# A fused decoder layer with its start, sample attention, norms and closing products rearranged

## The reference, cut to what matters

```
h   = rmsnorm(x, norm1_g) * (1 + sc1) + sh1        # sh, sc, gt: six parts of silu(c) @ ada_w + ada_b
z   = h @ w_in                                     # recurrent branch, queries, three K/V sets, gates
o_c = attention over compressed K/V (+ T5 bias)    # gelu(chunks of 32 rows @ cmp_w1) @ cmp_w2
o_s = attention over selected blocks,  o_w = attention over a window of 512
o_att = g0 * o_c + g1 * o_s + g2 * o_w             # sample requests read paged caches of 1,024 rows
mixed = concat(rmsnorm(o_lru), rmsnorm(o_att)) @ w_out
x   = x + gt1 * mixed
h2  = rmsnorm(x, norm2_g) * (1 + sc2) + sh2
x   = x + gt2 * peer_ffn(h2)                       # keys pick 16 of 16,384 experts per head
y   = rmsnorm(x, final_g)
```

## Time and profile before

| | us |
|---|---|
| median of 3 runs (lowest, highest) | 1961.47 (1959.98, 1966.07) |
| the profiled execution, its time | 1964.24 |
| its span, first to last instruction | 1962.6 |
| TensorE busy | 1802.6 (92%) |
| VectorE busy | 1327.0 (68%) |
| ScalarE busy | 647.5 (33%) |
| GpSimd busy | 337.4 (17%) |

### The profile page before, as it was taken

The page is one execution under the profiler, slowest core; times in us unless marked ns, Lnnn a source line. Parts: engine busy times, 40 slices in busy tenths (PEclk is TensorE's granted clock), DMA queues, the critical chain, the costliest instruction groups (busy, mean ns, idle before and its releaser), DMA issues.

```text
span 1962.6 us, 30207 instructions
## 1 busy us (share of the span) xinstructions
PE 1802.6 (92%) x11322; PEld 1670.6 (85%) x11322; DVE 1327.0 (68%) x2967; ACT 647.5 (33%) x1012; POOL 337.4 (17%) x362
## 2 busy tenths in 40 slices
PE   3889998757797999899999999999999999999996
PEld 2667785634586999899999999999999999999995
DVE  0310343347427778999999999995777777777775
ACT  1111332137313222333434334333333333333331
POOL 0301000000000000111123333432222222222220
PEclk9689998659998999999999999999999999999998
DMA  6573665230005322687679999998999999999981
GB/s 229 159 276 100 208 219 168 117 142 1 1 26 190 102 86 75 234 266 245 224 234 352 358 355 346 341 340 325 398 393 334 335 342 340 339 339 338 332 277 44
DMA packets 177773, 467.60 MB, mean 238 GB/s; under 512 B 20601, under 2 KB 91641, under 8 KB 175988
## 3 DMA queue, kind: packets, MB, share of 16 engines
q1 hardware_dynamic: 132788, 291.91, 42.8%
q0 software_dynamic: 44864, 174.14, 24.8%
HBM read 408.65 MB, written 64.14 MB: 241 GB/s over the span
## 4 chain that ended last, share of the span: by engine, by line
PE 83%; DVE 9%; DMA 4%; issue 2%; ACT 2%; SPq 0%; DVEq 0%; ACTq 0%; POOLq 0%
PE ps L1027 28%; PE ps L924 24%; PE ps L540 7%; PE ps L911 5%; PE ps L1008 4%; PE ps L873 3%; DMA arena<-rrows 1%; PE ps L592 1%; ACT arena L1061 1%; PE ps L563 1%; PE ps L849 1%; PE ps L549 1%; DMA cst<-in_rel_bias 1%; PE ps L841 1%; PE ps L898 1%
## 5 line engine op out<-in xcount | busy, mean ns | idle before, releaser
L1643 DVE TENSOR_TENSOR ul<-raw,uh 128x1024 fp32r<-128x1024 f32 x256 | 313.6, 1230 | 135.7 <-ACT uh L1061 117.5
L924 PE MATMUL ps<-hh,uh 128*128 128x392 f32 x1024 | 358.8, 350 | 5.8 <-DVE ul L1643 5.8
L1027 PE MATMUL ps<-ah,uh 128*128 128x392 f32 x1024 | 348.8, 341 | 2.7 <-DVE al L1848 2.7
L1027 PE MATMUL ps<-ah,ul 128*128 128x392 f32 x1024 | 350.9, 343 | 0.0
L1027 PE MATMUL ps<-al,uh 128*128 128x392 f32 x1024 | 350.2, 342 | 0.0
L924 PE MATMUL ps<-hl,uh 128*128 128x392 f32 x1024 | 350.0, 342 | 0.0
L924 PE MATMUL ps<-hh,ul 128*128 128x392 f32 x1024 | 349.0, 341 | 0.0
L1061 ACT ACTIVATE uh<-raw 128x1024 fp32r<-128x1024 f32 x256 | 270.3, 1056 | 116.4 <-PE ps L1027 106.1
L502 POOL DMA_INDIRECT xT<-in_u,gidx x128 | 148.2, 1158 | 591.1 <-DVE zg L1686 365.6
L502 POOL DMA_INDIRECT xT<-in_v,gidx x128 | 132.9, 1039 | 419.0 <-DVE vacc L1838 386.0
L924 PEld LDWEIGHTS ps<-hh,uh 128*128 128x128 f32 x1024 | 193.5, 189 | 8.7 <-DVE ul L1643 7.1
(11 more groups left out here) (326 smaller groups left out, 2270.8 us busy)
## 6 DMA issues: line engine op xcount, KB each, us to landing
raw<-in_uT SPq DMA_DIRECT2D x128, 512.0 KB
raw<-in_v SPq DMA_DIRECT2D x128, 512.0 KB
zs<-zbuf SPq DMA_DIRECT2D x128, 196.0 KB
gw<-stage POOLq DMA_DIRECT2D x28, 896.0 KB
gr<-gw SPq DMA_DIRECT2D x32, 784.0 KB, 9.0
zin<-zs SPq DMA_DIRECT2D x128, 196.0 KB
arena<-in_ada_w SPq DMA_DIRECT2D x32, 512.0 KB, 4.6
arena<-in_w_in SPq DMA_DIRECT2D x18, 512.0 KB, 4.4
```

The costliest lines, as they stand in the source:

```text
L924: last = mm(ps[:, bank, 0:DN], w[x][:, k * P:(k + 1) * P], m[:, k, G0:TOK], start=(k == 0 and x == 0 and m is hh), stop=(k == KD - 1 and x ...
L1027: last = mm(ps[:, dc, 0:DN], w[:, q, cols], m[:, q, :], start=(first and w is uh and m is ah), stop=(final and w is ul))
L1643: tt(ul[:, i % 4, :], raw[:, i % 4, :], uh[:, i % 4, :].bitcast(F32), SUB).then_inc(S["lo_done"], 1)
```

## The change

In the start, GpSimd's and SP's queues and TensorE's order are rearranged. The 55 bias products become eight, of which copies go out to memory (`obias`) and come back in shifted rows as `pbias`. SP loads 20 pages, GpSimd 44, the latter only after `ada_step(3)`. The replicated bias table `rbx` is made by a copy instead of a load. The eight products with `wgate` stand behind block 0 and use four column groups. Block 0 takes `h` chunk by chunk. `ohw`, the bias of the window, is loaded at block 5 instead of after block 17. `hidden_prompt(0)` stands behind `hidden_prompt(1)`. SP waits for `biasT` before it loads `wout`. Four norms (all but that of the recurrent branch) sum squares into four strips of 32 partitions, each for 128 prompt columns and 8 more (`SW` = 136), take inverse and root of 136 columns instead of 520, and spread the roots over all partitions by five products. The second norm goes chunk by chunk. The last three `down` steps are taken output by output, with the transposes in their middle.

```diff
+            load_head(1, 1)
...
-            load_head(1, 1)
...
-            load(rbx[0:32].rearrange("p (b h) -> p b h", h=NH),
-                 io["rel_bias"].rearrange("a (o h) -> a o h", o=1).to_broadcast([32, P // NH, NH]), S["tables_loaded"])
...
+            sp.wait_ge(S["ada_ready"], 3)
+            for n in range(2):
+                load(win_w[:, n * KD:(n + 1) * KD, :], io["w_in"][n], w_l[n])
...
-            sp.wait_ge(S["ada_ready"], 3)
-            for n in range(2):
-                load(win_w[:, n * KD:(n + 1) * KD, :], io["w_in"][n], w_l[n])
-            load(w1p, io["w1p"], S["w1k_loaded"])
-            load(posp, io["posp"], S["pos_loaded"])
...
-            load_pages(0, 16)
+            load_pages(0, 12)
+            load(w1p, io["w1p"], S["w1k_loaded"])
+            load(posp, io["posp"], S["pos_loaded"])
...
-                    load_pages(16, 32)
+                    load_pages(12, 16)
+                if n == 3:
+                    load_pages(16, 20)
+                if n == 5:
+                    load(ohw[0:33], io["ohw"], S["ohw_loaded"])
...
-            load(ohw[0:33], io["ohw"], S["ohw_loaded"])
...
             sp.wait_ge(S["sel_free"], 1)
+            sp.wait_ge(S["bias_loaded"], 16)
             load(wout, io["w_out"], S["wout_loaded"])
             load(xT[:, :, :], io["xT"], S["x_loaded"])
...
+            pool.wait_ge(S["act_init"], 3)
+            pool.dma_start(rscratch, rsb[0:NH]).then_inc(S["scratch_stored"], 16)
             pool.wait_ge(S["page_loaded"], 16)
-            pool.wait_ge(S["ada_ready"], 3)
-            for n in range(32, 64):
+            pool.wait_ge(S["ada_ready"], ADA_HEAD)
+            for n in range(20, 64):
...
+            ob = io["obias"]
+            for a in range(8):
+                pool.dma_start(bass.AP(ob.tensor, a * NH, [[64 * NH, 16], [8 * NH, 8], [1, NH]]),
+                               tofs[16 * a:16 * a + 16].rearrange("p (w h) -> p w h", h=NH)).then_inc(S["scratch_stored"], 16)
             rows = io["rrows"]
             pool.dma_start(rows.rearrange("p h c -> p (h c)"),
                            rscratch.rearrange("h (o c) -> o (h c)", o=1).to_broadcast([P, NH * 640])
                            ).then_inc(S["rows_stored"], 16)
+            pool.wait_ge(S["scratch_stored"], 16 * 9)
+            for a in range(8):
+                pool.dma_start(pbias[16 * a:16 * a + 16], bass.AP(ob.tensor, (7 - a) * NH, [[64 * NH, 16], [NH, QM], [1, NH]])
+                               ).then_inc(S["rows_stored"], 16)
...
+            def strip_sums(b, x, k, n):
+                for j in range(4):
+                    last = mm(ps[32 * j:32 * j + 32, b, 0:SW], ones[:, 0:32], x[:, k, j * P:j * P + SW],
+                              start=(k == 0), stop=(k == n - 1))
+                return last
+            def spread_roots(b, bs):
+                for j in range(4):
+                    mm(ps[:, b, j * P:(j + 1) * P], ident[:, 32 * j:32 * j + 1].to_broadcast([P, P]), roots[:, 0:P], start=True, stop=True)
+                mm(ps[:, bs, 256:256 + NB], ident[:, 96:97].to_broadcast([P, P]), roots[:, P:SW],
+                   start=True, stop=True).then_inc(S["roots_ready"], 1)
...
+                    pe.wait_ge(S["gather_k"], 16 * 20)
+                    pe.wait_ge(S["pages_k"], 16 * 44)
...
             for g in range(ADA_HEAD):
+                if g >= 1:
+                    turn_m9(g - 1)
+                if g == 2:
+                    pe.wait_ge(S["act_init"], 2)
+                    for k in range(KD):
+                        last = strip_sums(0, hT, k, KD)
+                    last.then_inc(S["sum_ready"], 1)
+                    pe.wait_ge(S["tables_loaded"], 80)
+                    mm(ps[0:NH, 2, 0:512], rb[0:33], ohd[0:33, 513:1025], start=True, stop=True)
+                    mm(ps[0:NH, 3, 0:128], rb[0:33], ohd[0:33, 1025:1153], start=True, stop=True)
+                    for w in range(KD):
+                        last = mm(ps[:, 3, P + w * NH:P + (w + 1) * NH], oha[0:33, w * P:(w + 1) * P], rb[0:33], start=True, stop=True)
+                    last.then_inc(S["pe_init"], 1)
+                if g == 3:
+                    pe.wait_ge(S["rstd_ready"], 1)
+                    spread_roots(1, 0)
                 pe.wait_ge(head_l[g % 3], 16 * (g // 3 + 1))
                 aw = ada_head[g % 3].rearrange("p (c k) i -> p c k i", k=KD)
                 ada_step(g, lambda k: aw[:, :, k, :], 512)
-                if g == 0:
-                    pe.wait_ge(S["tables_loaded"], 96)
-                    offset_bias(0)
-                    pe.wait_ge(S["act_init"], 2)
-                    two(0, lambda k: ones[:, :], lambda k: hT[:, k, :], range(KD)).then_inc(S["sum_ready"], 1)
-                    continue
-                turn_m9(g - 1)
-                if g == 3:
-                    pe.wait_ge(S["root_in"], 1)
-                    mm(ps[0:NH, 0, 0:512], rb[0:33], ohd[0:33, 513:1025], start=True, stop=True)
-                    mm(ps[0:NH, 1, 0:128], rb[0:33], ohd[0:33, 1025:1153], start=True, stop=True).then_inc(S["pe_init"], 1)
-                offset_bias(g)
...
+            def gate_strips():
+                pe.wait_ge(S["wgate_loaded"], 16)
+                pe.wait_ge(S["mt_done"], ADA_HEAD)
+                for kk in range(2):
+                    for h in range(2):
+                        for j in range(4):
+                            last = mm(ps[32 * j:32 * j + 32, 6 + h, 0:HALF], wgate[:, 2 * j + kk, :],
+                                      hT[:, 2 * j + kk, h * HALF:(h + 1) * HALF], start=(kk == 0), stop=(kk == 1))
+                last.then_inc(S["zg_ready"], 1)
...
+                for k in range(KD):
+                    if n == 0:
+                        pe.wait_ge(S["h_ready"], k + 1)
+                    for h in range(2):
+                        last = mm(ps[:, 2 * (n % 2) + h, 0:HALF], win_w[:, (n % 2) * KD + k, :],
+                                  hT[:, k, h * HALF:(h + 1) * HALF], start=(k == 0), stop=(k == KD - 1))
...
-                    last.then_inc(S["zg_ready"], 1)
+                    gate_strips()
+                if n == 1:
+                    gate_sums()
...
+            hidden_prompt(1, 7, 128)
+            pe.wait_ge(S["w1k_loaded"], 48)
+            hidden_prompt(0, 1, 160)
...
+            pe.wait_ge(S["gelu_ready"], 4)
             pe.wait_ge(S["att_dve"], 3)
...
-            hidden_prompt(0, 160)
...
-            for c in range(2):
-                project(c, range(4))
+            project(0, range(4))
             pe.wait_ge(S["mix_sq"], 1)
-            two(0, lambda k: ones[:, :], lambda k: hT[:, k, :], range(4)).then_inc(S["mix_sum"], 1)
+            for k in range(4):
+                last = strip_sums(0, hT, k, 4)
+            last.then_inc(S["mix_sum"], 1)
+            project(1, range(3))
+            pe.wait_ge(S["rstd_ready"], 3)
+            spread_roots(1, 0)
+            project(1, range(3, 4))
             project(2, range(4))
             pe.wait_ge(S["mix_ready"], 1)
...
+                if c >= 2:
+                    chunk_sums(x1sq, c - 2, 0, 0)
+            for k in range(KD - 2, KD):
+                chunk_sums(x1sq, k, 0, 0)
+            pe.wait_ge(S["rstd_ready"], 4)
+            spread_roots(2, 3)
...
+                    if ready is not None and k % 2 == 0:
+                        pe.wait_ge(ready, k // 2 + 1)
...
+            down(P - 4, 0)
+            for dc in range(KD):
+                cols = slice(dc * P, (dc + 1) * P)
+                for q in range(1, 4):
+                    if dc == 0:
+                        pe.wait_ge(S["lo_done"], 2 * P - 3 + q)
+                        pe.wait_ge(S["a_ready"], P - 3 + q)
+                    for w, m in ((uh, ah), (uh, al), (ul, ah)):
+                        last = mm(ps[:, dc, 0:DN], w[:, q, cols], m[:, q, :], start=False, stop=(q == 3 and w is ul))
+                last.then_inc(S["ff_ready"], 1)
+                if dc == 3:
+                    pe.wait_ge(S["acc_step"], P)
+                    pe.wait_ge(S["bank_free"], 2)
+                    for c in range(KD):
+                        last = pe.transpose(ps[:, c // 4, (c % 4) * P:(c % 4 + 1) * P], vacc[:, c * P:(c + 1) * P], ident[:, :])
+                    last.then_inc(S["pe_turned"], 1)
+            for k in range(KD):
+                chunk_sums(sq, k, KD, 2)
+            pe.wait_ge(S["rstd_ready"], 5)
+            spread_roots(3, 2)
...
-            act.wait_ge(S["h_ready"], 2 * KD)
-            fn(hh[:, :, :], h2T, ACT.Copy).then_inc(S["rounded"], 1)
...
+            for k in range(KD):
+                act.wait_ge(S["h_ready"], KD + k + 1)
+                fn(hh[:, k, :], h2T[:, k, :], ACT.Copy).then_inc(S["hh_ready"], 1)
...
+            link(cp(rbx[0:33].rearrange("p (b h) -> p b h", h=NH),
+                    rb[0:33].rearrange("p (o h) -> p o h", o=1).to_broadcast([33, P // NH, NH])))
...
+            shift_m(1)
+            dve.wait_ge(S["sum_ready"], 1)
```

(44 more changed lines are left out.)

195 lines of the change are left out of this document (86 added, 109 removed).

## The result

The changed kernel takes 1863.74 us (median of four runs, 1859.92 to 1866.52) against 1960.72 (1958.52 to 1966.07) in the same series: a ratio of 0.950, 95% interval 0.9472 to 0.9528, 97 us less. Forecast were 1862, range 1844 to 1884.

A forecast was written before the change was run, and what follows sets the result against it. TensorE, 83% of the chain, was taken as the bound, with gains only in the first 620 and last 30 us. Gains 40 + 35 + 7 + 5 + 13 = 100 gave 1862 us, own range 1850 to 1874, wider range 1844 to 1884.

The forecast's parts named there:

- Term 1: Start: page products begin at 103 instead of 144.6, with GpSimd's queue of pages as bound; gain 40 us, bounds 33 to 49.
- (a): Start: GpSimd's pages come slower than 1.18, at 1.6 each, so 44 cost 19 us more: 1881; chance 0.12.
- (e): Start: it gains nothing because transfers bound it, so the time is 1902; chance 0.03.
- Term 2: Sample attention: earlier `ohw`, reordered products and `biasT` travelling alone gain 35 us, bounds 27 and 42.
- (b): Sample attention: `biasT` is slow by itself, nearly 25 even alone, so gain 20 instead of 35: 1877; chance 0.13.
- Term 3: Mix norm: the 4.26 wait goes and the square sums shrink; gain 7 us, bounds 5 and 8.
- Term 4: Second norm: the split, held by the last expert row's transfer, starts earlier; gain 5 us, bounds 2 and 8.
- Term 5: End: outputs ready one by one and shorter square sums and inverse gain 13 us, bounds 10 and 15.
- (c): Sample products and start: less idling keeps the clock's upper level, 8 to 12 us more gain: 1852; chance 0.12.
- (d): Expert loop: granted clock falls because TensorE comes warmer, making it slower than before; at 0.90, 2006 us; chance 0.02.

The follow-up runs named there:

- the split of 28 to 36: Changed kernel with 28 pages on SP's queue and 36 on GpSimd's instead of 20 and 44: 1855.72 us, ratio 0.9452.
- the added line: Kernel before with one line added, SP waiting for `biasT` before loading `wout`: 1941.79 us against 1963.47, ratio 0.9899.
- the two other parts: Two runs on the changed kernel: `hidden_prompt(0)` back behind the turning products, 1867.89 us; `ohw` loaded after the projection's last block again, 1864.69 us.

## Why the prediction was right

**Term 1, 40 us: right in sum (38) and in what set the time, but two of its sizes were wrong and cancel, which is luck.** The start of the page products was put at 47 + 1.5 + 52 + 2.7 = 103. In the changed kernel's profile it is 39.9 + 1.6 + 50.4 + 8.9 = 100.8, and on the mean of the executions 104.2. The step that set the term, GpSimd's 44 pages at 1.18 (measured 1.17), was right, and the split of 28 to 36 shows it: the bound goes with it. The fourth `ada_step` came earlier than 47, by 7.1 in the profile and by 3.3 on the mean of nine. The term chose the low clock and supported it with a misreading: in the earlier trace rows the slice from 49 us stands at 6 and the next at 8, not at nine tenths with 0.6 and 0.5 behind; rows of several executions show that both levels occur. The last page came later: 8.6 after its issue instead of 2.7. The 2.7 of the earlier trace rows is the median of 32 pages, and the last of them had already taken 5.4 before the change. TensorE's list from the fourth step, which did not set the time, was put at 48 (95 less 47) and took 55: `w_in` for block 2 was issued only at 57.6, behind SP's 12 pages, for a wait of 2.76 and a block of 10.14 instead of 7.28. That SP's share of the pages delays the weights was not in the working. In passing, 55 bias products at the rate of the first 14 make 24 us and not 21; the four groups took 21.4 in the trace, two of them faster. Of the 38, some 27 lie ahead of the end of the fourth `ada_step`, where the wait for the bias table is gone, and 13 behind it, less 2.4 in the page products. No run undid a part of the new start by itself, so the shares of the table, the bias products, the gates and the queues are read from the rows and not shown by experiment.

The rival of slower pages (a) fails on the interval. The Trainium skill, "SBUF — State Buffer", section "SBUF: two separate sides", has VectorE lock GpSimd out of writing descriptors in some modes; VectorE was busy for 7.6 of the 10 us from 40, and the interval there stays at 1.16 but for one of 1.5 (in every profile of the changed kernels the eighth interval is that long), so the trace does not show it at work here; whether VectorE was in such a mode is not shown either. The rival that transfers bound the start (e) fails as a bound, though they are near: 398 GB/s moved between 90 and 101 us, just ahead of the page products.

**Term 2, 35 us: right (34).** The rearranged products brought `sel_free` 16.0 us forward within the stage, where the working had 15.6. `biasT` landed in 8.9, inside the 7.3 to 14.5, and the added line alone wins 22 on the kernel before; rival (b) falls. Undoing the two other parts costs 5.6 and up to 6.8. The working had 7.8 for the order of `hidden_prompt(0)`: part of that was a wait for VectorE that now hides the moved products, made up by the clock of the scores behind. The Trainium skill, "DMA: Bandwidth & Descriptors", section "Queues, rings and completion order", has each DMA engine take turns between queue rows by packet. The prediction took this as equal shares of bytes and saw the trace disagree. Counted in the profile's packets, the trace comes near it while `wout` moved: 138 packets of GpSimd's queue against 188 of SP's, of 4 KB against 26 KB, so that `biasT` got a tenth of the bytes. Behind `wout`, until `biasT` landed, the counts are 390 against 804, so turns were not equal throughout. Whether the profile's packets are those of the page is not shown, and no run changed their size: that the size of the packets decides is argued, not shown.

**Term 3, 7 us: right (6).** The wait is gone, sums take 1.13, spreading 1.05 and 0.29. No run undid this part by itself.

**Term 4, 5 us: right (5), with its reason.** The raw row set the time: VectorE waits 3.84 for ScalarE, which had waited for `uT` until 514.57, and rounding `hh` first gives 3.6 more.

**Term 5, 13 us: right (14).** With the strip norm kept, undoing the order of outputs costs 7.8, and some six are left for the norm, where the working had 3.8 and some 9. That is no contradiction: the last sums start 2.2 behind the last product (2.0 in the working), but they are short (0.44, 0.4 in the working) only because the other seven chunks are summed while the last is made. So 3.9 us belong to both edits together.

**The other rivals.** The clock (c) came half: the start gained some 3 by it on the mean (43.7 against 47). (d) fails: the experts took 1313.8 against 1312.1. The spans of the profiled pair differ by 104 and the medians by 97: in the profiled execution the fourth `ada_step` ended 3.7 ahead of the mean of nine and the sample attention took 2.5 less than its mean.

## What to carry to other kernels

When two transfers start together and only one is waited for, hold the other back with a wait: one line won 22 of 1,963 us here. A queue that needs several instructions for each small transfer has a rate of its own (1.17 us a page); count what stands on each queue, and what weights stand behind it, before moving work from one to the other. On an engine that rounds or copies for others, put first what comes first, and last what still waits for memory.
